# Two-block transformer on one core: the order of weight tiles in the mixers and in the output projection

## The chip, the cores and the metric

The kernel runs on one core of one Trainium2 chip, written in Bass with hand-placed semaphores. The metric is device time in microseconds of one execution; the median of three runs of the kernel before is 2701.41 us (2698.37 to 2704.88).

## The reference, cut to what matters

Two blocks of two layers each work on x of 256 tokens by 1024 features in float32. The change touches the token mixers of both. In each, three branches are weighted by gates, summed and projected:

```python
# first block, per layer (heads 8, head width 64; latent widths 256 and 128)
y_a = from_heads(moba_attention(partial_rope(qa), partial_rope(ka), va))
y_b = from_heads(stick_breaking_attention(qb_, kb_, vb_))
qc = to_heads(rms_norm(c_q, q_norm) @ w_uq, MLA_HEADS)
kv = to_heads(rms_norm(c_kv, kv_norm) @ w_ukv, MLA_HEADS)
kr = apply_rope(k_rope, cos_m, sin_m)              # one rotary key for all heads
y_c = from_heads(causal_softmax_attention(qc, concat(k_nope, kr), vc))
g = sigmoid(gates + b_gate)
merged = sum over n of g[n] * (y_n @ w_branch[n])
return merged @ w_out

# second block, per layer
o_b = rmsnorm(diff attention output, subln_g) * (1 - lambda_init)
u, v = gelu(uv);  v = rmsnorm(v, norm_g)
o_c = u * (einsum('gts,bnsgc->bntgc', tril(w_s), v) + b_s)   # the gating unit
mixed = gates[0] * (o_a @ w_branch_a) + gates[1] * (o_b @ w_branch_b) + gates[2] * (o_c @ w_branch_c)
x = x + mixed @ w_out
```

## The kernel before

Activations lie features by tokens: 128 partitions, 8 chunks of 256 tokens. Weights come as a stream of 360 tiles of 128x2048 (1 MB), built on the host in the order in which they are used (`weight_tiles`), through a ring of three slots. SyncE loads a slot as soon as VectorE is through with its last tile; ScalarE rounds the tile to its high part (`split_high`, L937), VectorE subtracts to get the low part (`split_low`, L1366), and TensorE makes three products for each block of 128x128: high by high, high by low, low by high (`blocks`, L374 to L376). A tile is 16 blocks, 48 matmuls over 256 tokens.

There is no scheduler. Each engine runs a program of its own, in the order written, and they meet on counted semaphores. `split_ahead` and `tile_done` let ScalarE and VectorE run up to three tiles ahead; both stand at fixed places in their programs. A projection (`project`, L419) takes the next tile and writes one of PSUM's banks 4 and 5 in turn (`open_fill`, L388); it waits until ScalarE has taken the bank's last result (`take`, L966; semaphore `pj_out`).

In the mixers, projections run beside attention steps. `sticks(beside)` (L512) is the stick-breaking attention: step s makes head s's scores, then calls `beside(s)`, then the running sums of head s-1 and the weighted values of head s-3. VectorE adds the sums (L1534) and the mask (L1541), ScalarE makes exp (L1046) and the log in three operations (L1052 to L1056). In step 0 comes the tile of the rotary key and the latent norms (high and low parts of the small operand, L1184 and L1764); in step 1 the query latent (`mla_w_uq`: four banks), and the rotation of the key, `kr`, held in `ff[64:96, 0, :]`; in step 2 the key/value latent (`mla_w_ukv`: six banks) and the first query rotation; in steps 3 to 8 the gate and branch tiles of branch 0 (`merge_gate`, `merge_branch`), with three more query rotations. A rotation is a matmul with a permutation to bank 6 (`rotate`, L437) and three VectorE operations (`rope`, L1465 to L1468), and it waits for the last rotation's `rope_done`. A branch result of half the features fills banks 6 and 7, and VectorE multiplies it by the gates held in `ff` (`merge_step`).

In the second block, behind the diff attention, come the norm of its output (two statistics, each two matmuls into bank 6, L896; ScalarE's `root`, L986 and L988; VectorE's scaling, L1911), the norm and products of the gating unit (L1916 and L903), and then the gate and branch tiles of branches 1 and 2.

The output projection (L571) multiplies four tiles by the merged input, whose second half of features is ready last (`merged_part`, L1583; semaphore `ml_ready`, counted once for each half). Its results lie in banks 0 to 3.

## Time and profile before

| | us |
|---|---|
| median of 3 runs | 2701.41 |
| profiled execution | 2703.62 |
| its span | 2702.0 |
| TensorE busy | 2451.9 |
| VectorE busy | 1662.1 |
| ScalarE busy | 1214.4 |

Mean granted clock of TensorE over the span: 0.946. The page lists busy time by engine, the waits name who held whom, the timeline shows single instructions with the idle time before them. The time in an idle bracket is counted from the end of the last instruction's record; matmuls overlap, so in dense code one starts before the last one's record ends.

### The profile page before, as it was taken

The numbers are of one execution on the slowest core, as the hardware profiler recorded it, in microseconds if no ns is written. First come the engines' busy times: TensorE is split into PE (matmuls) and PEld (weight loads), VectorE is DVE, ScalarE is ACT, GpSimd is POOL, SyncE is SP. The second block draws the span as 40 slices with busy tenths as digits, with TensorE's granted clock in tenths as the row PEclk, the third lists the DMA queues.
The fourth block names the chain that finished last, engine by engine and source line by source line (L and its number), as shares of the span: only waits on it lengthen the run. The fifth ranks groups of instructions, "written<-read, shape, count | busy, mean of one in ns | idle before, by whom it ended". The sixth has DMA issues, their size and how long they took to land.

```text
span 2702.0 us, 43597 instructions
## 1 busy us (share of the span) xinstructions
PE 2451.9 (91%) x16380; PEld 2198.0 (81%) x16380; DVE 1662.1 (62%) x2378; ACT 1214.4 (45%) x1574; POOL 73.4 (3%) x141
## 2 busy tenths in 40 slices
PE   3998989979979989899799898989899889988998
PEld 2997978869968978788789787679799876888897
DVE  6876656656768776665565554445655555555654
ACT  3444455444444444554344454354444443454443
POOL 0100000000000000000000000000000000000000
PEclk9998989989999999999999987899999988989999
DMA  7775544436647764444345433134455331334452
GB/s 302 276 277 174 185 164 163 163 122 220 246 171 250 277 235 156 173 155 159 138 156 186 171 127 108 63 125 162 160 182 183 139 141 63 126 125 156 170 181 100
DMA packets 74141, 461.52 MB, mean 171 GB/s; under 512 B 8272, under 2 KB 8416, under 8 KB 27648
## 3 DMA queue, kind: packets, MB, share of 16 engines
q1 hardware_dynamic: 53424, 384.33, 39.8%
q0 software_dynamic: 19120, 70.43, 7.4%
q10 hardware_dynamic: 1440, 4.62, 0.4%
q8 instruction: 104, 1.70, 0.3%
q14 instruction: 53, 0.43, 0.1%
HBM read 458.30 MB, written 1.05 MB: 170 GB/s over the span
## 4 chain that ended last, share of the span: by engine, by line
PE 85%; DVE 6%; ACT 4%; issue 3%; DMA 1%; DVEq 1%; ACTq 0%; SPq 0%
PE ps L594 19%; PE ps L374 16%; PE ps L375 16%; PE ps L376 16%; PE ps L596 9%; PE ps L431 2%; PE ps L491 1%; PE ps L442 1%; PE ps L458 1%; DMA set_a<-in_ada 1%; PE ps L471 1%; PE ps L457 1%; ACT whi L937 1%; DVE wlo L1366 1%; DVE x L1451 1%
## 5 line engine op out<-in xcount | busy, mean ns | idle before, releaser
L1366 DVE TENSOR_TENSOR wlo<-raw,whi 128x2048 fp32r<-128x2048 f32 x360 | 824.4, 2291 | 321.1 <-ACT whi L937 301.4
L937 ACT ACTIVATE whi<-raw 128x2048 fp32r<-128x2048 f32 x360 | 687.5, 1910 | 295.4 <-PE ps L376 292.1
L594 PE MATMUL ps<-hx,whi 128*128 128x512 f32 x2112 | 764.7, 405 | 33.0 <-DVE hx L1439 27.6
L596 PE MATMUL ps<-hx,wlo 128*128 128x256 f32 x2112 | 597.8, 283 | 0.0
L374 PE MATMUL ps<-hx,whi 128*128 128x256 f32 x1680 | 504.1, 300 | 27.0 <-DVE hx L1583 14.5
L594 PEld LDWEIGHTS ps<-hx,whi 128*128 128x128 f32 x2112 | 400.7, 190 | 141.8 <-DVE hx L1439 38.4
L375 PE MATMUL ps<-hx,whi 128*128 128x256 f32 x1680 | 486.9, 290 | 0.0
L376 PE MATMUL ps<-hx,wlo 128*128 128x256 f32 x1680 | 486.2, 289 | 0.0
L374 PE MATMUL ps<-yhi,whi 128*128 128x256 f32 x1440 | 408.5, 284 | 0.0
L375 PE MATMUL ps<-ylo,whi 128*128 128x256 f32 x1440 | 407.5, 283 | 0.0
L376 PE MATMUL ps<-yhi,wlo 128*128 128x256 f32 x1440 | 407.3, 283 | 0.0
L596 PEld LDWEIGHTS ps<-hx,wlo 128*128 128x128 f32 x2112 | 404.3, 191 | 0.0
L374 PEld LDWEIGHTS ps<-hx,whi 128*128 128x128 f32 x1680 | 333.1, 198 | 47.8 <-DVE hx L1583 15.3
L375 PEld LDWEIGHTS ps<-hx,whi 128*128 128x128 f32 x1680 | 334.1, 199 | 4.6 <-issue 4.4
L376 PEld LDWEIGHTS ps<-hx,wlo 128*128 128x128 f32 x1680 | 333.7, 199 | 0.0
L374 PEld LDWEIGHTS ps<-yhi,whi 128*128 128x128 f32 x1440 | 275.8, 192 | 4.7 <-issue 1.4
L376 PEld LDWEIGHTS ps<-yhi,wlo 128*128 128x128 f32 x1440 | 276.1, 192 | 0.0
L375 PEld LDWEIGHTS ps<-ylo,whi 128*128 128x128 f32 x1440 | 276.0, 192 | 0.0
L1391 DVE CUSTOM_DVE_ANT_0 adat<-adat,cact 128x1024 f32<-128x1024 f32 x128 | 155.4, 1220 | 5.0 <-issue 4.5
L1110 ACT ACTIVATE set_b<-ps 128x512 f32<-128x512 f32 x66 | 39.5, 599 | 238.5 <-PE ps L596 238.5
L431 PE MATMUL ps<-set_a,const 128*128 128x256 f32 x136 | 48.3, 516 | 97.2 <-DVE set_a L1419 97.2
L431 PEld LDWEIGHTS ps<-set_a,const 128*128 128x128 f32 x136 | 32.6, 255 | 108.8 <-DVE set_a L1419 70.4
(245 smaller groups left out, 2602.5 us busy)
## 6 DMA issues: line engine op xcount, KB each, us to landing
raw<-in_w SPq DMA_DIRECT2D x360, 1024.0 KB, 4.8
adat<-in_ada POOLq DMA_DIRECT2D x128, 512.0 KB, 4.5
raw<-in_ada SPq DMA_DIRECT2D x4, 512.0 KB, 11.3
blk<-in_block POOLq DMA_DIRECT2D x2, 990.5 KB, 5.0
set_a<-in_ada SPq DMA_DIRECT2D x3, 512.0 KB, 25.1
raw<-in_ada ACTq DMA_DIRECT2D x2, 512.0 KB, 11.8
set_b<-in_ada ACTq DMA_DIRECT2D x2, 512.0 KB, 17.5
x<-in_x SPq DMA_DIRECT2D x1, 1024.0 KB, 18.6
```

The source lines that it names most:

```text
L374: mm(out_ap, sh, mh, start=start and first, stop=False, skip_group_check=skip)
L375: mm(out_ap, sh, ml, start=False, stop=False, skip_group_check=skip)
L376: last = mm(out_ap, sl, mh, start=False, stop=stop and end, skip_group_check=skip)
L431: last = mm(stat[:, 0, :], c("inv1024"), sq[:, i // 2 * 4 + i % 2, :], start=(i == 0), stop=(i == 3))
L442: mm(out_ap, perm, src, start=True, stop=True).then_inc(*T.counts("rot_ready"))
L457: mm(ps[:, bank, 0:128], ins.q(u, 0, 128), ins.k(u, 0, 128), start=True, stop=True)
L594: mm(ps[:, bank + i, :].rearrange("p (a s) -> p a s", a=2), whi[:, slot, col:col + P], hx[:, :, k, :], start=(k == 0), stop=False)
L596: last = mm(ps[:, bank + i, 0:S], wlo[:, slot, col:col + P], hhi[:, k, :], start=False, stop=(k == KD - 1))
L937: A(whi[:, slot, :], raw[:, slot, :], ACT.Copy).then_inc(*T.counts("hi_ready"))
L1110: A(gate_sum, ps[:, 4:6, S:2 * S], ACT.Copy).then_inc(*T.counts("gb_ready"))
L1366: tt(wlo[:, slot, :], raw[:, slot, :], whi[:, slot, :].bitcast(F32), ALU.subtract)\
L1391: nc.vector.tensor_tensor_reduce(adat[:, slot, :], adat[:, slot, :], cact[:, :], 1.0, 0.0, ALU.mult, ALU.add, out_ap).then_inc(*T.counts(" ...
```

## The change

Output projection, both blocks: the first-half products of tiles 0 and 1 (both column groups) are made before the wait for the merged input's second half; the second halves follow. The two column groups of a bank now form one accumulation, as `down` does it.

First block: the tile stream and the steps beside the stick-breaking attention are reordered to rotary key, gate, query latent, gate, key/value latent, branch. The query rotations move: 0 after the gate tile of step 3; 1, 2 and 3 inside the key/value latent. The rotary key is held in `merged[64:96, 7, :]`, since gate results now fill `ff` before it has been used.

Second block: one gate tile before the sub-norm's statistics and one after them; the second statistic goes to bank 7 and no longer waits for the first root; ScalarE and VectorE each split one weight tile ahead of the first root. The first two gate tiles of the later loop are left out.

```diff
--- before.py
+++ after.py
@@ -279,7 +279,7 @@
 
         pos_in = bufC[:, 0, 0:S].bitcast(I32)
         cq_raw = set_a[:, 12:15, :]
-        kr = ff[64:96, 0, :]
+        kr = merged[64:96, 7, :]
         gs = ff[:, :, :]
         a32 = ff[:, 2:4, :]
         gate_sum = set_b[:, 0:2, :]
@@ -569,17 +569,28 @@
                 pe.wait_ge(*T.nth("y_ready", T.n["pairs"]))
 
             def output_projection():
+                def part(i, slot, half):
+
+                    for j in range(2):
+                        last = blocks(acc[:, 2 * i + j, :],
+                                      [(whi[:, slot, k * 256 + j * P:k * 256 + (j + 1) * P],
+                                        wlo[:, slot, k * 256 + j * P:k * 256 + (j + 1) * P],
+                                        hhi[:, k, :], hlo[:, k, :]) for k in range(4 * half, 4 * half + 4)],
+                                      start=(half == 0 and j == 0), stop=(half == 1), skip=True)
+                    return last
+
+
+                pe.wait_ge(*T.next("ml_ready"))
+                slots = []
+                for i in range(2):
+                    slots.append(tile())
+                    part(i, slots[i], 0)
+                pe.wait_ge(*T.next("ml_ready"))
                 for i in range(4):
-                    slot = tile()
-                    for j in range(2):
-                        for half in range(2):
-                            if i == j == 0:
-                                pe.wait_ge(*T.next("ml_ready"))
-                            last = blocks(acc[:, 2 * i + j, :],
-                                          [(whi[:, slot, k * 256 + j * P:k * 256 + (j + 1) * P],
-                                            wlo[:, slot, k * 256 + j * P:k * 256 + (j + 1) * P],
-                                            hhi[:, k, :], hlo[:, k, :]) for k in range(4 * half, 4 * half + 4)],
-                                          start=(half == 0), stop=(half == 1))
+                    if i >= 2:
+                        slots.append(tile())
+                        part(i, slots[i], 0)
+                    last = part(i, slots[i], 1)
                     last.then_inc(*T.counts("tile_used"))
 
 
@@ -687,7 +698,11 @@
                         mm(stat[:, 1, :], c1("inv128"), sq[:, 2, :], start=True, stop=True)\
                             .then_inc(*T.counts("stat_ready"))
                         free6[0] = None
-                    elif s == 1:
+                    elif s in (1, 3, 6, 7):
+                        merge_gate()
+                        if s == 3:
+                            rotate_q(0)
+                    elif s == 2:
                         slot = tile()
                         wait_h(3)
                         for i in range(4):
@@ -702,7 +717,7 @@
                             last.then_inc(*T.counts("tile_used" if i == 3 else "part_ready"))
                         pe.wait_ge(*T.nth("pj_out", T.n["fills"] - 4))
                         rotate(c1("perm_mla")[64:96, 64:128], kr, ps[64:128, 6, 0:S])
-                    elif s == 2:
+                    elif s == 4:
                         slot = tile()
                         for i in range(4):
                             bank = open_fill()
@@ -712,6 +727,8 @@
                                               [(whi[:, slot, col:col + P], wlo[:, slot, col:col + P],
                                                 smallhi[:, 512:768], smalllo[:, 512:768])])
                             last.then_inc(*T.counts("part_ready"))
+                            if i == 1:
+                                rotate_q(1)
                         for t in range(2):
                             bank = open_fill()
                             wv = [w_[:, slot, 0:1024].rearrange("p (h c) -> p h c", c=P)[:, :, HD:P]
@@ -720,18 +737,11 @@
                                           [(smallhi[:, 512 + t * P:512 + (t + 1) * P],
                                             smalllo[:, 512 + t * P:512 + (t + 1) * P], wv[0], wv[1])])
                             last.then_inc(*T.counts("tile_used" if t == 1 else "part_ready"))
-                        rotate_q(0)
-                    elif s < 9:
-                        if s in (3, 4):
-                            rotate_q(s - 2)
-                        if s % 3 == 2:
-                            if s == 5:
-                                wait_bank6()
-                            merge_branch(0)
-                        else:
-                            merge_gate()
-                        if s == 4:
-                            rotate_q(3)
+                            rotate_q(2 + t)
+                    elif s in (5, 8):
+                        if s == 5:
+                            wait_bank6()
+                        merge_branch(0)
 
                 sticks(beside_sticks)
                 wait_pairs()
@@ -886,15 +896,15 @@
                             merge_gate()
 
                 attend(diff, beside_diff)
+                merge_gate()
                 wait_bank6()
-
                 for i in range(2):
                     pe.wait_ge(*T.next("sq_ready"))
-                    if i:
-                        pe.wait_ge(*T.nth("rstd_ready", T.n["stat_ready"]))
                     for j in range(2):
-                        last = mm(stat[:, j, :], c2("inv128"), sq_od[:, 2 * i + j, :], start=True, stop=True)
+                        last = mm(ps[:, 6 + i, j * S:(j + 1) * S], c2("inv128"), sq_od[:, 2 * i + j, :],
+                                  start=True, stop=True)
                     last.then_inc(*T.counts("stat_ready"))
+                merge_gate()
 
                 pe.wait_ge(*T.next("vs_ready"))
                 pe.wait_ge(*T.next("wt_ready"))
@@ -908,8 +918,9 @@
                 free6[0] = None
                 for n in (1, 2):
                     for half in range(2):
-                        merge_gate()
-                        merge_gate()
+                        if (n, half) != (1, 0):
+                            merge_gate()
+                            merge_gate()
                         if n == 2 and half == 0:
                             pe.wait_ge(*T.next("gl_ready"))
                         merge_branch(n)
@@ -980,10 +991,10 @@
             def use_exp_tanh():
                 act.preload_act_table_set("exp_and_others")
 
-            def root(n=1):
+            def root(n=1, bank=6):
 
                 act.wait_ge(*T.next("stat_ready"))
-                A(rstd[:, 0:n, :], stat[:, 0:n, :], ACT.Ln, bias=c("eps"))
+                A(rstd[:, 0:n, :], ps[:, bank, 0:n * S].rearrange("p (c s) -> p c s", c=n), ACT.Ln, bias=c("eps"))
                 act.drain()
                 A(rstd[:, 0:n, :], rstd[:, 0:n, :], ACT.Exp, scale=-0.5).then_inc(*T.counts("rstd_ready"))
 
@@ -1183,14 +1194,16 @@
                             act.wait_ge(*T.next("t2_ready"))
                             A(smallhi[:, i * S:(i + 1) * S], set_a[:, 4 + i, :], ACT.Copy)\
                                 .then_inc(*T.counts("hh_ready"))
-                    elif s == 1:
+                    elif s in (1, 3, 5, 6, 7, 8):
+                        merge_step({1: 0, 3: 1, 5: 2, 6: 0, 7: 1, 8: 2}[s], 0, s // 6, True)
+                    elif s == 2:
                         for i in range(4):
                             if i < 3:
                                 act.wait_ge(*T.next("part_ready"))
                             else:
                                 tile_done()
                             take(set_a[0:96, 2 * i:2 * i + 2, :], rows=96)
-                    elif s == 2:
+                    elif s == 4:
                         for i in range(4):
                             act.wait_ge(*T.next("part_ready"))
                             take(set_a[0:64, 8 + 2 * i:10 + 2 * i, :], rows=64)
@@ -1199,8 +1212,6 @@
                         tile_done()
                         take(vm[:, 1, :])
                         act.wait_ge(*T.next("kr_ready"))
-                    elif s < 9:
-                        merge_step(s % 3, 0, s // 6, True)
 
                 sticks(1, beside_sticks)
 
@@ -1319,8 +1330,9 @@
                 A(rsum[:, 0, :], rsum[:, 0, :], ACT.Ln, bias=c("eps"), scale=1.0 / 512)
                 act.drain()
                 A(rsum[:, 0, :], rsum[:, 0, :], ACT.Exp, scale=-0.5).then_inc(*T.counts("vr_ready"))
+                split_high()
                 for i in range(2):
-                    root(2)
+                    root(2, 6 + i)
                     for j in range(2):
                         act.wait_ge(*T.next("odt_ready"))
                         A(yhi[:, 1, 2 * i + j, :], odt[:, 2 * i + j, :], ACT.Copy, scale=lam[:, 5:6])\
@@ -1764,22 +1776,21 @@
                             tt(smalllo[:, i * S:(i + 1) * S], set_a[:, 4 + i, :],
                                smallhi[:, i * S:(i + 1) * S].bitcast(F32), ALU.subtract)\
                                 .then_inc(*T.counts("h_ready"))
-                    elif s == 1:
+                    elif s in (1, 3, 5, 6, 7, 8):
+                        merge_step({1: 0, 3: 1, 5: 2, 6: 0, 7: 1, 8: 2}[s], 0, s // 6, True)
+                        if s == 3:
+                            rope_q(0)
+                    elif s == 2:
                         tile_done(False)
                         T.n["pj_out"] += 4
                         rope(kr, kr, ps[64:96, 6, 0:S], cosm, sinm, rstd[64:96, 0, :])
                         nc.vector.tensor_copy(set_a[64:96, 8:16, :], over(kr, HEADS))\
                             .then_inc(*T.counts("kr_ready"))
-                    elif s == 2:
+                    elif s == 4:
                         tile_done(False)
                         T.n["pj_out"] += 6
-                        rope_q(0)
-                    elif s < 9:
-                        if s in (3, 4):
-                            rope_q(s - 2)
-                        merge_step(s % 3, 0, s // 6, True)
-                        if s == 4:
-                            rope_q(3)
+                        for i in (1, 2, 3):
+                            rope_q(i)
                     if s < 8:
                         last_modulation(8 + s)
 
@@ -1905,6 +1916,7 @@
                 v.wait_ge(*T.next("vq_ready"))
                 tt(rsum[:, 0, :], esum[:, :, 0], esum[:, :, 1], ALU.add).then_inc(*T.counts("vsum_ready"))
                 T.n["sq_ready"] += 2
+                split_low()
                 for i in range(2):
                     root()
                     for j in range(2):
@@ -2084,8 +2096,8 @@
                 down(j - 1)
         down(NJ - 1)
 
-    def merge(gates, g0, branch, n_):
-        for half in range(2):
+    def merge(gates, g0, branch, n_, halves=(0, 1)):
+        for half in halves:
             put(slab(gates, g0 + n_ * D + 512 * half))
             put(slab(gates, g0 + n_ * D + 512 * half + 256))
             put(slab(branch, 512 * half, 512))
@@ -2099,9 +2111,13 @@
         put(slab(w, c_q))
         put(slab(w, c_kv, P))
         put(slab(w, k_r - 64, 96))
+        put(slab(w, gates))
         put(slab(inp["mla_w_uq"][l], 0, HEADS * MLA_QK))
+        put(slab(w, gates + 256))
         put(slab(inp["mla_w_ukv"][l], 0, HEADS * P))
-        for b in range(3):
+        put(slab(inp["mix_w_branch"][l, 0], 0, 512))
+        merge(w, gates, inp["mix_w_branch"][l, 0], 0, (1,))
+        for b in (1, 2):
             merge(w, gates, inp["mix_w_branch"][l, b], b)
         for j in range(4):
             put(slab(inp["mix_w_out"][l], 256 * j))
```

## Rows read from the trace of the kernel before

**Rows 1.** Page, part 1: engine, busy us (share of the span), instructions.

```profile
PE 2451.9 (91%) x16380; PEld 2198.0 (81%) x16380; DVE 1662.1 (62%) x2378; ACT 1214.4 (45%) x1574; POOL 73.4 (3%) x141
```

**Rows 2.** Waits of PE, whole span: who <- releaser: us in total, times, longest.

```profile
PE ps L431 <- DVE set_a L1419: 97.2, 17, 28.6
...
PE ps L374 <- DVE hx L1583: 14.5, 4, 3.6
...
PE ps L374 <- ACT set_a L966: 9.0, 2, 4.5
```

**Rows 3.** Timeline, PE, output projection: start us, us, instruction, count [idle before <- releaser].

```profile
551.51 0.28 PE L375 MATMUL ps<-hx,whi 128*128 128x256 f32 x1
551.63 0.28 PE L376 MATMUL ps<-hx,wlo 128*128 128x256 f32 x1
555.53 0.39 PE L374 MATMUL ps<-hx,whi 128*128 128x256 f32 x1 [3.62 <-DVE hx L1583]
```

**Rows 4.** Windows: stretch, us, busy us (count) by engine, PEclk, DMA share, GB/s.

```profile
555.50:578.90 23.40, 23.36 (x180) 23.16 (x180) 10.97 (x10) 7.67 (x5) 0.53 (x1) 0.93 0.47 161
2466.20:2490.40 24.20, 24.11 (x180) 23.90 (x180) 9.23 (x5) 7.62 (x4) 0.00 (x0) 0.89 0.38 132
```

**Rows 5.** Timeline, DVE, around the output projection's start.

```profile
548.38 2.29 DVE L1366 TENSOR_TENSOR wlo<-raw,whi 128x2048 fp32r<-128x2048 f32 x1 [0.58 <-ACT whi L937]
...
554.25 1.23 DVE L1583 SCALAR_TENSOR_TENSOR hx<-merged,hx 128x1024 fp32r<-128x1024 f32 x1 [1.12 <-ACT hx L1090]
```

**Rows 6.** Timeline, PE, second block: end of attention to first branch tile.

```profile
1807.74 0.38 PE L492 MATMUL ps<-bufC,set_b 128*128 128x128 f32 x2
1810.13 1.13 PE L896 MATMUL ps<-set_a,blk 128*128 128x256 f32 x4 [2.01 <-ACT set_a L973]
1816.54 2.07 PE L896 MATMUL ps<-set_a,blk 128*128 128x256 f32 x4 [5.28 <-ACT rstd L988]
1821.67 3.79 PE L903 MATMUL ps<-blk,set_a 128*128 128x128 f32 x16 [3.06 <-DVE set_a L1916]
1825.11 0.56 PE L374 MATMUL ps<-hx,whi 128*128 128x256 f32 x1
1825.47 0.41 PE L375 MATMUL ps<-hx,whi 128*128 128x256 f32 x1
1825.68 0.41 PE L376 MATMUL ps<-hx,wlo 128*128 128x256 f32 x1
...
1837.21 0.28 PE L374 MATMUL ps<-yhi,whi 128*128 128x256 f32 x1
```

**Rows 7.** Timeline, ACT and DVE, the same stretch.

```profile
1804.47 2.29 DVE L1366 TENSOR_TENSOR wlo<-raw,whi 128x2048 fp32r<-128x2048 f32 x1 [4.41 <-ACT whi L937]
...
1815.11 0.68 ACT L986 ACTIVATE rstd<-ps,const 128x512 f32<-128x512 f32 x1
...
1820.75 0.87 DVE L1916 TENSOR_SCALAR set_a<-set_a,rsum 128x512 f32<-128x512 f32 x2
...
1828.63 2.29 DVE L1366 TENSOR_TENSOR wlo<-raw,whi 128x2048 fp32r<-128x2048 f32 x1 [0.17 <-issue]
```

**Rows 8.** Timeline, PE, stick-breaking attention of the first layer.

```profile
374.95 0.36 PE L374 MATMUL ps<-smallhi,whi 128*96 128x256 f32 x1 [3.20 <-DVE smalllo L1764]
...
390.95 0.58 PE L374 MATMUL ps<-smallhi,whi 128*128 128x256 f32 x1 [4.49 <-ACT set_a L966]
...
396.26 1.07 PE L442 MATMUL ps<-set_a,blk 32*64 32x512 f32 x2
...
399.66 0.61 PE L442 MATMUL ps<-set_a,blk 32*64 32x512 f32 x1 [0.41 <-DVE set_a L1468]
...
419.75 0.39 PE L374 MATMUL ps<-yhi,whi 128*128 128x256 f32 x1
```

**Rows 9.** Timeline, DVE and ACT, step 2 of the same attention.

```profile
386.91 0.56 DVE L1534 TENSOR_TENSOR bufA<-bufA,ps 128x384 f32<-128x384 f32 x1
...
390.32 1.05 ACT L966 ACTIVATE set_a<-ps 64x512 f32<-64x512 f32 x2
```

## Prediction

> **What bounds the kernel now.** I read the page's busy times first: TensorE is busy for 2451.9 of 2702.0 us [rows 1], so it sets the end and an edit is worth what it takes out of TensorE's 250 idle us, plus what the clock gives back. Then the waits of TensorE over the whole span [rows 2]: the largest group, 97.2 us before the mean over x, is a chain of norms that the change doesn't touch. Those that it touches are the output projection's second wait (14.5 us, 4 times) and, in each of the two layers of a block, three more: the sub-norm's second statistic waits 5.3 us for the first root [rows 6], and in the stick-breaking attention the latent projections wait 3.2 us for the small operand's low part [rows 8] and 4.5 for a bank to be taken (9.0 in both). Last I read the timeline around one of each, since a wait is only worth its length if the next thing is ready, and the granted clock behind it.
>
> **What an idle TensorE costs twice.** In dense code a 128x256 matmul follows the last one after 0.12 us (551.51 to 551.63, [rows 3]). The 180 matmuls behind the output projection's wait would then take 179 x 0.12 + 0.28 = 21.76 us; they took 23.36, at a mean clock of 0.93, and in the fourth place 24.11 at 0.89 [rows 4]. So a wait of 3.6 us is followed by a stretch at the lower level (1.2 of 2.4 GHz) that costs 1.6 us once or 2.35 in the fourth place. Where the wait goes, that goes too.
>
> **Part 1, output projection (4 places).** Before, 12 matmuls (first half of output tile 0, j = 0) run, then TensorE stands from 551.63 + 0.12 = 551.75 to 555.53, 3.78 us, for the second half of the merged input's low part [rows 3]. The change puts all 48 first-half matmuls of the first two weight tiles ahead of that wait: 36 more, 36 x 0.12 = 4.32 us. They end at 551.75 + 4.32 = 556.07, 0.54 us after the wait's end, so it is covered whole. What must hold: the second tile's low part. VectorE makes it from 548.38 to 550.67 and the merged half from 554.25 to 555.48 [rows 5]; TensorE wants the second tile at 550.32 + 24 x 0.12 = 553.2, so it is 2.5 us early. Nothing is added: the number of matmuls, and the banks that they use, stay; the tile that is handed back first is used up at 559.0 instead of 559.9, so the ring isn't held either. Gain: 4 x 3.78 = 15.1 us of waits, and 3 x 1.6 + 2.35 = 7.15 us of clock, **22.3 us**. Bounds: 15.1 (the low stretches reappear at the next work) to 22.3.
>
> **Part 2, gating unit of the second block (2 places).** Before: statistic 1 starts at 1810.13 after 2.01 us idle, statistic 2 at 1816.54 after 5.28, the gating products at 1821.67 after 3.06, gate tiles 1 and 2 at 1825.11, and the first branch tile at 1837.21 [rows 6]. After: TensorE is free at about 1808.05 (the last attention product starts at 1807.74 and dense code follows it 0.31 later). Gate tile 1 takes 48 x 0.12 = 5.8 us, to 1813.9; both statistics, now in two banks, need the squares (there by 1810.7) and no root between them: 8 instructions, 2.07 us for 4 at the low clock [rows 6], so 1.7 for 8 at the full one and up to 3.5 at the low one; to 1815.6. Gate tile 2 goes to 1821.4. The later of the two gate tiles was split by 1804.47 + 2.29 = 1806.8 [rows 7], ahead of all this.
> The side that gets longer is ScalarE and VectorE. The change lets each split one weight tile (1.91 and 2.29 us by the page's groups) ahead of the first root. ScalarE's Ln is at 1815.11 [rows 7], so it moves to 1816.9 and its Exp ends at 1818.3; VectorE's split, which needs ScalarE's, runs 1817.0 to 1819.25, so the first normed pair starts then, 2.7 us later than before. From there the chain of before again, without its wait for statistic 2: Ln at 1820.6, root at 1822.0, the second pair 1822.1 to 1822.7, the scaled values to 1823.6 (before, 1820.75 to 1821.62 [rows 7]). So the gating products wait until 1823.65: TensorE idles 2.25 us there instead of 3.06, and this is the new last wait. The products took 3.44 us at the low clock (1821.67 to 1825.11), so 1.75 at the full one; then the branch tile starts at 1825.4, against 1837.21, a gain of 11.8 us. The low parts that the branch needs end at 1825.2. If the clock is low behind the 2.25 us, the products cost 1.7 more and a piece of the next tile up to 1.6. I take 10.5 for each place, **21 us**; bounds 2 x 8.5 to 2 x 12. The split brought forward is free otherwise: before, it stood at 1828.63 [rows 7], behind the gating unit, and the following tiles (1829 to 1831, 1831 to 1833) stay just ahead of TensorE, which wants the first at 1831.2.
>
> **Part 3, latent projections in the stick-breaking attention (2 places).** Order before, by step: key rotary tile; query latent; key/value latent; then gate, gate, branch. After: rotary tile; gate; query latent; gate; key/value latent; branch. The same matmuls run between the end of step 1's scores (374.95 less the wait before it, 371.7) and the branch tile (419.75), so the difference of its start is the gain [rows 8]. Walking it by the rows of before: gate 1 fills 371.7 to 377.5, over the 3.20 us wait. The running sums and scores end at 379.35, the query latent's first two banks (12 matmuls each) at 382.2. The third bank needs ScalarE's first take, and ScalarE makes it behind its own step: argument, exp, masked scores, three-op log. From VectorE's argument (386.91) to the end of the first take (390.32 + 0.59 = 390.91) that is 4.0 us [rows 8, 9]. VectorE reaches the argument at 380.4 (tile split to 379.15, modulation unit 1.2), the take ends at 384.4: a wait of 2.3 us that wasn't there. The key rotation and the next step end at 389.7, gate 2 at 395.5. VectorE rotates query 0 and does its unit, so the argument of step 4 is at 400.3 and the first key/value take ends at 404.3; TensorE has done two banks and a rotation by 401.5 and waits 2.8 (before 4.49). The query rotations 2 and 3 now sit inside that tile, and one follows another by 3.40 at the least (396.26 to 399.66 [rows 8]), since each waits until VectorE is through the last: waits of 0.4 and 1.8. The branch tile starts at 414.0. That is 5.75 us less if the clock stays up; gaps of 2.3 and 2.8 us with rotations around them should leave one or two low stretches, 2 us. **3.75 each, 7.5 us**; bounds 0 (three low stretches and a take 1 us later) to 11.5. The moved rotary key is the same copy and rotation to another place in SBUF, and its copy ends (390.6) long before it is read: nothing. Seven query, key and gate tiles change places in the stream of 1 MB loads, whose landing takes 4.8 us by the page; each is issued when the slot's low part is done, and the latest, that of the branch tile, lands some 20 us ahead: nothing.
>
> **Sum.** 22.3 + 21 + 7.5 = 50.8 us. The profiled execution took 2703.62 us, 1.6 over its span; this gives 2652.8 for it, and **2651** against the median of 2701.41.
>
> **Rivals.** (a) Part 3 brings nothing, because the ScalarE to VectorE chain comes last in both latent steps, and the smaller gaps leave as many low stretches as before. For it: my walk already finds 7.3 us of gaps where 8.1 stood. With part 2 at its lower bound of 17 us it gives 22.3 + 17 = 39.3, so 2662. Chance 0.25. (b) The gaps that are left don't lower the clock: the wait of 2.01 us before statistic 1 still had its matmuls at short spacing (4 in 1.13 us). Then 22.3 + 23.6 + 11.5 = 57.4, so 2644. Chance 0.12. (c) **Slower.** The granted clock. The long waits become more and shorter ones, and if each then holds TensorE low through what follows, not for a stretch but for the whole step, part 3's 36 us of work and part 2's 17 us per layer run at 0.21 us (1825.47 to 1825.68, [rows 6]) for 0.12: (36 + 17) x 0.75 = 40 us a layer, 80 in all, against 50.8 gained: 2731. It decides from some 26 us of added loss per layer. Against it: dense tiles bring the clock back soon: the 96 matmuls from 1825.11 to 1837.21 take 12.1 us, 0.6 over 96 x 0.12 [rows 6]. Chance 0.015. The Trainium skill, "TensorE: Matmul & The Clock Gate", section "A second HAM failure mode: psum-queue depth-cycling", states the rule that speaks for (c): short idle times between groups of matmuls that cycle through banks can make the clock swing between its levels. Taken at its word it would leave 2731; the low stretches of this trace follow idle or sparse TensorE time only. (d) The change doesn't do what it says: TensorE doesn't reach the filler because a tile or bank isn't ready. It would cost part 2's gain and half of part 1, leaving 18: 2683. The splits speak against it [rows 5, 7]. Chance 0.015. The forecast keeps 0.6.
>
> **Range and chances.** Forecast's own range 2645 to 2658; with (a) and (b), **2642 to 2667**. A measurement of this kernel can tell about 0.2%, 5.4 us, from no change. Faster by more: 0.97 (forecast, a, b); within: 0.015; slower: 0.015.
>
> **What would show it.** Right: no wait on the merged low part in the output projection, and some 192 matmuls in 23.1 us there; the root's wait gone, one wait of 2 to 2.5 us before the gating products; in the latent steps no wait on the small operand's low part, two of 2 to 3 us on ScalarE's takes, one near 1.8 us on the third rotation; mean clock up from 0.946. Wrong if the gating products wait 4 us or more, if the takes come as late as before (4.5 us), or if low stretches appear inside the dense gate tiles.

## The result, and the profile after

The changed kernel takes a median of 2656.0 us in four runs (2654.7 to 2663.0), beside 2701.1 us (2698.4 to 2704.9) for the kernel before on the same chip: a ratio of 0.9837, 95% interval 0.9816 to 0.9859, or 45 us less by the medians. (The ratios here and below are those on record with the runs; a quotient of medians can differ from them by 0.001.) The forecast was 2651 us, the range 2642 to 2667. The profiled execution is the longest of the four: 2663.0 us, its span 2661.4, against 2703.62 and 2702.0 before. So the traces differ by 40.6 us, and the terms below are held against that, not against 45.

The changed kernel's page, part 1 (as [rows 1]), and its waits of PE over the span (as [rows 2]):

```profile
PE 2448.2 (92%) x16380; PEld 2189.4 (82%) x16380; DVE 1660.7 (62%) x2378; ACT 1212.6 (46%) x1574; POOL 73.0 (3%) x141
```

```profile
PE ps L431 <- DVE set_a L1431: 97.2, 17, 28.7
...
PE ps L374 <- ACT set_a L977: 8.5, 4, 2.4
...
PE ps L913 <- DVE set_a L1928: 4.4, 2, 2.2
...
PE ps L442 <- DVE set_a L1480: 2.0, 2, 1.3
```

The output projection's wait (14.5 us, 4 times, in [rows 2]) has no row any more. What is left of the three parts is what the forecast's walk left: two waits of 2.2 us before the gating products, four on ScalarE's takes of the latent results, and two on a rotation. TensorE is busy for as long as before (2448.2 us against 2451.9), so nearly all that was won is idle time.

**Output projection**, timeline of PE, and the row of VectorE that was waited for before (against [rows 3, 5]):

```profile
547.97 0.28 PE L374 MATMUL ps<-hx,whi 128*128 128x256 f32 x1
...
553.73 0.28 PE L374 MATMUL ps<-hx,whi 128*128 128x256 f32 x1
...
573.16 0.67 PE L431 MATMUL ps<-set_a,const 128*128 128x256 f32 x2 [1.99 <-DVE set_a L1431]
```

```profile
551.91 1.22 DVE L1595 SCALAR_TENSOR_TENSOR hx<-merged,hx 128x1024 fp32r<-128x1024 f32 x1 [1.13 <-ACT hx L1101]
```

The low part of the merged input's second half is ready at 553.13; the second halves begin at 553.73, when the 48 first halves are through, without an idle bracket. The wait is covered with 0.6 us to spare.

**Gating unit**, timeline of PE in the first layer, of its last row in the second, and of ACT and DVE (against [rows 6, 7]):

```profile
1798.35 0.60 PE L491 MATMUL ps<-bufC,set_b 128*128 128x256 f32 x2
...
1804.75 1.89 PE L904 MATMUL ps<-set_a,blk 128*128 128x256 f32 x8
...
1814.60 2.05 PE L913 MATMUL ps<-blk,set_a 128*128 128x128 f32 x16 [2.21 <-DVE set_a L1928]
1816.40 0.37 PE L374 MATMUL ps<-yhi,whi 128*128 128x256 f32 x1
...
2363.29 3.68 PE L913 MATMUL ps<-blk,set_a 128*128 128x128 f32 x16 [2.21 <-DVE set_a L1928]
2366.63 0.45 PE L374 MATMUL ps<-yhi,whi 128*128 128x256 f32 x1
```

```profile
1806.17 1.91 ACT L948 ACTIVATE whi<-raw 128x2048 fp32r<-128x2048 f32 x1
1807.98 0.67 ACT L997 ACTIVATE rstd<-ps,const 128x512 f32<-128x512 f32 x1
...
1808.11 2.29 DVE L1378 TENSOR_TENSOR wlo<-raw,whi 128x2048 fp32r<-128x2048 f32 x1 [4.48 <-ACT whi L948]
...
1813.66 0.88 DVE L1928 TENSOR_SCALAR set_a<-set_a,rsum 128x512 f32<-128x512 f32 x2
```

Both statistics run as one group of 8, and the root comes behind the split on ScalarE. The same stretch in the kernel before begins in the first layer, and begins and ends in the second, at

```profile
1807.30 0.60 PE L491 MATMUL ps<-bufC,set_b 128*128 128x256 f32 x2
...
2373.07 0.60 PE L491 MATMUL ps<-bufC,set_b 128*128 128x256 f32 x2
...
2403.35 0.28 PE L374 MATMUL ps<-yhi,whi 128*128 128x256 f32 x1
```

From the last L491 group to the branch tile it is 18.05 us in the first layer (before, 1807.30 to 1837.21: 29.91) and 19.59 in the second (from 2347.04; before, 30.28), where the same 16 gating products take 3.34 us to the next tile instead of 1.80, at the low clock.

**Latent projections**, timeline of PE (against [rows 8]):

```profile
381.52 0.36 PE L374 MATMUL ps<-smallhi,whi 128*96 128x256 f32 x1 [1.88 <-ACT set_a L977]
...
401.70 0.58 PE L374 MATMUL ps<-smallhi,whi 128*128 128x256 f32 x1 [2.36 <-ACT set_a L977]
402.51 0.41 PE L374 MATMUL ps<-smallhi,whi 128*128 128x256 f32 x1
...
405.84 1.96 PE L442 MATMUL ps<-set_a,blk 32*64 32x512 f32 x2
...
410.04 1.94 PE L442 MATMUL ps<-set_a,blk 32*64 32x512 f32 x2 [0.65 <-DVE set_a L1480]
...
415.38 1.22 PE L518 MATMUL ps<-set_b 64*128 64x256 f32 x2
...
416.96 0.58 PE L374 MATMUL ps<-yhi,whi 128*128 128x256 f32 x1
```

The three waits have the places and nearly the lengths of the walk. What it lacked is the clock. Behind 401.70 each group of three matmuls takes 0.64 us (402.51 to the next at 403.15), and a pair of rotation matmuls (405.84) 1.96 instead of the 1.07 of [rows 8]: the lower of the two levels, 1.2 of 2.4 GHz. It stays low until the branch tile has run for 4 us (at 421.4 a group takes 0.36 again), some 20 us in all.

**The windows** of PE show it by stage: us, busy us (count) of PE, PEld, DVE, ACT, POOL, then granted clock, DMA share and GB/s. First two output projections, then the two gating units, then the two latent stages (from the second step's scores to the branch tile behind the sixth's):

```profile
547.90:571.10 23.20, 23.20 (x194) 23.07 (x193) 15.03 (x14) 10.00 (x6) 0.53 (x1) 1.00 0.62 210
2424.40:2447.70 23.30, 23.29 (x195) 23.09 (x193) 13.22 (x8) 10.00 (x6) 0.00 (x0) 1.00 0.53 185
1798.30:1816.40 18.10, 15.89 (x126) 15.42 (x125) 7.91 (x14) 13.65 (x27) 0.00 (x0) 1.00 0.33 117
2347.00:2366.60 19.60, 17.39 (x126) 16.92 (x125) 7.91 (x14) 15.16 (x27) 0.00 (x0) 0.92 0.31 108
368.00:417.00 49.00, 44.11 (x238) 33.46 (x237) 34.16 (x49) 26.55 (x41) 2.64 (x5) 0.83 0.42 149
1123.20:1172.40 49.20, 43.63 (x237) 34.12 (x236) 34.17 (x49) 26.48 (x41) 2.63 (x5) 0.86 0.39 139
```

And the latent stages of the kernel before, which the rows ahead of the prediction don't cover as a window:

```profile
370.80:419.70 48.90, 40.80 (x237) 33.39 (x236) 32.70 (x46) 26.05 (x41) 2.12 (x4) 0.90 0.38 137
1126.20:1174.50 48.30, 40.21 (x237) 33.04 (x236) 32.68 (x46) 26.04 (x41) 2.12 (x4) 0.89 0.40 145
```

The same work, with TensorE 3.3 us longer "busy" and as much less idle: the waits that went were paid back at the clock.

### The profile page after: what moved, and what is told of

The parts are those of the page before. It is cut to its first block, busy times and chain, and to the rows that moved or that the text cites. A ratio compares the mean times of both kernels' runs of the same rounds, so it can differ in the third digit from the quotient of the medians.

```text
span 2661.4 us, 43595 instructions
## 1 busy us (share of the span) xinstructions
PE 2448.2 (92%) x16380; PEld 2189.4 (82%) x16380; DVE 1660.7 (62%) x2378; ACT 1212.6 (46%) x1574; POOL 73.0 (3%) x141
## 4 chain that ended last, share of the span: by engine, by line
PE 86%; DVE 5%; ACT 4%; issue 3%; DMA 1%; DVEq 1%; ACTq 0%; SPq 0%
PE ps L605 19%; PE ps L374 16%; PE ps L375 15%; PE ps L376 15%; PE ps L607 9%; PE ps L431 2%; PE ps L491 1%; PE ps L442 1%; PE ps L458 1%; DMA set_a<-in_ada 1%; PE ps L471 1%; PE ps L457 1%; ACT whi L948 1%; DVE x L1463 1%; PE ps L492 1%
## 5 line engine op out<-in xcount | busy, mean ns | idle before, releaser
L605 PEld LDWEIGHTS ps<-hx,whi 128*128 128x128 f32 x2112 | 400.7, 190 | 141.8 <-DVE hx L1451 38.4
L374 PE MATMUL ps<-hx,whi 128*128 128x256 f32 x1680 | 498.8, 297 | 13.0 <-DVE hx L1451 5.4
L375 PE MATMUL ps<-hx,whi 128*128 128x256 f32 x1680 | 481.5, 287 | 0.0
L374 PEld LDWEIGHTS ps<-hx,whi 128*128 128x128 f32 x1680 | 327.4, 195 | 30.3 <-issue 10.5
L375 PEld LDWEIGHTS ps<-hx,whi 128*128 128x128 f32 x1680 | 328.5, 196 | 4.5 <-issue 4.4
## 6 DMA issues: line engine op xcount, KB each, us to landing
raw<-in_ada ACTq DMA_DIRECT2D x2, 512.0 KB, 11.8
```

Source lines behind the costliest of these rows:

```text
L374: mm(out_ap, sh, mh, start=start and first, stop=False, skip_group_check=skip)
L375: mm(out_ap, sh, ml, start=False, stop=False, skip_group_check=skip)
L605: mm(ps[:, bank + i, :].rearrange("p (a s) -> p a s", a=2), whi[:, slot, col:col + P], hx[:, :, k, :], start=(k == 0), stop=False)
```

## The experiments

The theory (A) was: parts 1 and 2 give what was forecast; part 3 gives nothing, because its smaller waits still bring the clock down, and now in a stage of small matmuls where that costs more. Its rival (B): part 3 gives its 7.5 us, and the missing microseconds are lost elsewhere. The first four runs do one part each, and one takes part 3's waits away. Each batch of runs has its own median of the kernel before: 2699.17, 2700.82 and 2699.54 us.

**One part alone: the output projection.** The kernel before with only `output_projection` of the change.

```diff
+                pe.wait_ge(*T.next("ml_ready"))
+                for i in range(2):
+                    slots.append(tile())
+                    part(i, slots[i], 0)
+                pe.wait_ge(*T.next("ml_ready"))
```

> The kernel before with the output projection's new order alone. Both theories: the wait for the merged low part and the low clock behind it go in all four places, 5.4, 5.4, 5.4 and 6.1 us in the profiled execution, together 22.3, so 2679 against 2701. A ratio of 0.9917. If it gives less than 18 us, the reordered work has a price that the stage does not show.

Measured: 2682.56 us, ratio 0.9943 (0.9927 to 0.9958), 16.6 us less. From the first of its 192 matmuls to the mean over x each place gains what it gains in the whole change: 5.37, 5.37, 5.38 and 6.16 us, 22.3 in all. So the stage is as forecast, and by the medians some 6 us are lost outside it. The windows of the norms behind two of these stages show a part of it: first the kernel before, then this one.

```profile
577.90:612.00 34.10, 21.80 (x95) 16.22 (x94) 20.29 (x34) 17.21 (x27) 0.00 (x0) 0.85 0.19 63
1332.60:1367.00 34.40, 22.22 (x92) 16.90 (x91) 20.17 (x33) 16.76 (x26) 0.00 (x0) 0.80 0.18 62
```

```profile
568.30:602.40 34.10, 22.09 (x92) 16.48 (x91) 20.16 (x33) 16.60 (x26) 0.00 (x0) 0.70 0.17 62
1319.30:1353.70 34.40, 22.39 (x93) 16.81 (x93) 20.25 (x34) 17.15 (x27) 0.00 (x0) 0.70 0.18 64
```

The same norm code, at a granted clock of 0.70 instead of 0.85 and 0.80. From the first mean to the second it takes 9.91 us instead of 9.40 in the first place, and in the five such stages together 2.5 us more. No edit touches them. The rest of the loss stands in no trace: this profiled execution is the fastest of its six, 24.6 us below the profiled one of before, and 4.9 us of that come from the second block's first layer between its first norm and its output projection (339.8 us before, 334.9 here), which no edit touches either.

**One part alone: the gating unit.**

```diff
                 attend(diff, beside_diff)
+                merge_gate()
                 wait_bank6()
...
-                    if i:
-                        pe.wait_ge(*T.nth("rstd_ready", T.n["stat_ready"]))
...
+                merge_gate()
```

> The kernel before with the second block's part alone (gate tiles around the statistics, statistic 2 in bank 7, one tile split ahead of the first root). From the changed kernel's profile: 11.8 us less in the first layer's stretch, 10 to 12 in the second's, together 22 to 24, so 2678. Rival: the wait of 2.2 us that is left before the gating products keeps the clock low in some executions, and the gain is 19 to 20.

Measured: 2681.94 us, ratio 0.994 (0.9923 to 0.9956), 17.2 us less. Timeline of PE, first layer:

```profile
1817.70 3.68 PE L903 MATMUL ps<-blk,set_a 128*128 128x128 f32 x16 [2.21 <-DVE set_a L1919]
1821.11 0.39 PE L374 MATMUL ps<-yhi,whi 128*128 128x256 f32 x1
```

The wait of 2.21 us stands where it was forecast, and here the clock is low behind it in both layers: 19.66 us to the branch tile (from 1801.45), as in the second layer of the whole change. That is a gain of 10.3 us in the first layer and 10.7 in the second (2357.77 to 2377.38). Some 3.7 us of these 20.9 do not reach the median. The profiled execution (2679.57) doesn't show the loss, being 24 us below the profiled one of before, so what took them is not settled.

**One part alone: the latent projections.** The tile stream, the rotary key's place and the steps of the first block; of the edit, the two gate tiles in the stream:

```diff
+        put(slab(w, gates))
         put(slab(inp["mla_w_uq"][l], 0, HEADS * MLA_QK))
+        put(slab(w, gates + 256))
         put(slab(inp["mla_w_ukv"][l], 0, HEADS * P))
```

> The kernel before with the latent part alone (tile order, gate tiles between the latent projections, rotations inside the key/value latent, rotary key moved). Theory A, from the changed kernel's profile: the waits fall from 8.1 to 4.9 or 5.6 us in a layer, but rotations, takes and short waits leave TensorE sparse and the clock low for 10 to 20 us, so a layer gains nothing or loses 2: 2699 to 2705. Theory B, my forecast: 7.5 us gained, 2694, and what was missing from the forecast lies elsewhere in the clock.

Measured: 2699.88 us, ratio 1.0005 (0.9992 to 1.0018), twelve runs from 2691.9 to 2710.5. No gain (the interval leaves room for 2 us), and not the 7.5 of theory B: theory A. Its profile holds both outcomes. Timeline of PE in the first layer, and the windows of the stage in both:

```profile
383.15 0.36 PE L374 MATMUL ps<-smallhi,whi 128*96 128x256 f32 x1 [1.88 <-ACT set_a L965]
...
403.35 0.39 PE L374 MATMUL ps<-smallhi,whi 128*128 128x256 f32 x1 [2.36 <-ACT set_a L965]
```

```profile
369.70:412.20 42.50, 36.83 (x234) 29.35 (x233) 31.78 (x45) 25.04 (x39) 2.11 (x4) 1.00 0.46 163
1118.60:1167.50 48.90, 44.02 (x234) 33.84 (x233) 33.19 (x46) 25.04 (x39) 2.11 (x4) 0.81 0.41 149
```

The same two waits as in the changed kernel, to a hundredth, and in the first layer the clock stays up: from the second step's scores to the sixth's 42.47 us, against 48.08 before. In the second layer of the same execution it falls, and the stretch takes 48.88 us and the two steps behind it 2.56 more. So up to the eighth step the order is worth 5.6 us a layer if the clock holds and costs up to 4 if it doesn't.

**The waits of part 3 taken away.** In steps 2 and 4 ScalarE takes the first latent bank before its own exp and the second one before it waits for the masked scores, so that TensorE's third bank is free; and the query rotations 2 and 3 move out of the key/value latent to steps 6 and 7.

```diff
             for s in range(HEADS + 3):
                 split_ahead()
+                early(s, 0)
...
                     A(bufC[:, u % 2, :], bufA[:, u % 2, :], ACT.Exp).then_inc(*T.counts("w_ready"))
+                early(s, 1)
...
                     elif s in (1, 3, 6, 7):
                         merge_gate()
+                        if s >= 6:
+                            rotate_q(s - 4)
...
-                            rotate_q(2 + t)
                     elif s in (5, 8):
-                        if s == 5:
-                            wait_bank6()
+                        wait_bank6()
```

> The changed kernel, with ScalarE taking the first two banks of each latent tile ahead of its exp and its log instead of behind them, and with query rotations 2 and 3 moved out of the key/value latent to behind the gate tiles of steps 6 and 7. Theory A (the takes and the rotations set these stages, and the low clock follows the waits that they leave): the waits of 1.9 and 2.4 us and that of 0.7 to 1.3 before the third rotation go, and so do low stretches of 10 to 15 us in a layer, worth 5 to 7: 8 to 10 us a layer, 2656 becomes 2638 to 2642. Theory B (the walk was right and the low stretches are chance): only the waits go, 4.5 us a layer, 2647. Rival C: the chain of exp and log gets later by the two takes (0.6 us each), and TensorE waits for the running sums instead: no change, 2656.

Measured: 2638.63 us, ratio 0.9775 (0.9759 to 0.9791), below either kernel. Windows of the two latent stages and their last wait on a take:

```profile
367.50:403.20 35.70, 34.96 (x233) 29.77 (x232) 29.38 (x42) 25.62 (x41) 2.11 (x4) 1.00 0.55 196
1109.30:1145.00 35.70, 34.96 (x233) 29.78 (x232) 29.37 (x42) 25.64 (x41) 2.11 (x4) 1.00 0.57 197
```

```profile
399.13 0.50 PE L374 MATMUL ps<-whi,smallhi 128*128 128x512 f32 x1 [0.74 <-ACT set_a L977]
```

The stage takes 34.8 us instead of 47.3, at the full clock; the next two steps take 18.1 instead of 19.5, with two rotations more in them. Of the 12.5 us in the first layer 4.8 are the clock (47.3 against the 42.5 of the layers in which it held), 4.8 are waits (those of a layer in which it held, 1.88 + 2.36 + 1.33, less 0.74), and the rest is mostly the two pairs of rotation matmuls that now run later.

**Only the early takes** (the two calls of `early` in the diff above), and **only the spread rotations** (its second half), to see which of the two it is.

> The changed kernel with ScalarE's early takes alone; the three query rotations stay inside the key/value latent. Theory (takes and rotations each set a wait): the waits of 1.9 and 2.4 us go, those for the rotations stay and grow, since TensorE reaches them 2 us earlier and VectorE does not: one wait of 2 to 3 us more in the key/value latent, some 3 to 5 us gained per layer with part of the low clock, 2647. Rival (the takes were all of it, the rotations cost nothing): as the version with both edits, 2639.

Measured: 2653.15 us, ratio 0.9815 (0.9797 to 0.9832). The waits on the takes are gone but for one of 0.74 us, and the rotations are late instead, since VectorE (L1490) has not finished the one before:

```profile
403.76 1.04 PE L442 MATMUL ps<-set_a,blk 32*64 32x512 f32 x2 [1.73 <-DVE set_a L1490]
...
407.03 1.94 PE L442 MATMUL ps<-set_a,blk 32*64 32x512 f32 x2 [0.93 <-DVE set_a L1490]
```

The second pair takes 1.94 us for the first one's 1.04: two waits, 1.73 and 0.93 us, and the clock is low again through the end of the step. 42.7 and 42.9 us for the stage.

> The changed kernel with query rotations 2 and 3 moved to behind the gate tiles of steps 6 and 7, and the takes left where they are. Theory: the waits of 1.9 and 2.4 us stay, the wait of 0.7 to 1.3 before the third rotation goes, and TensorE's work between the waits gets denser behind the key/value latent, so the long low stretch shortens: 3 to 4 us gained per layer, 2649. Rival (only the takes count): 2656.

Measured: 2653.94 us, ratio 0.9817 (0.98 to 0.9834). Both waits on the takes stand (1.87 and 2.36 us). The stage takes 39.8 us in the first layer and 42.5 in the second, with 3.4 and 10.2 us at the low clock.

Against the changed kernel (0.9837, and 0.9845 when it ran again) each alone gives some 0.0025 of the ratio, 7 us; both together give 0.007, 18. In the stage itself it is 4.7 and 6.3 us a layer for each alone and 12.7 for both (means of the two layers, from 47.5). With the two steps behind it, in which the moved rotations run, it is 5.7, 7.5 and 13.8. So the two mostly add up. What both give over the sum (1.7 us a layer in the stage, 0.6 with the two steps) fits the clock, which is low for some of the stage while either kind of wait is left and nowhere once both are gone, but the medians can't tell 14 from 18. Nor does all of it arrive: from the eighth step's scores to the output projection the kernels with the moved rotations take 114.7 to 117.3 us, the changed kernel 112.8 and 113.1. They have a wait of 0.5 to 0.6 us on a rotation before a branch tile there, and some of them a low stretch more.

**The gating unit without the split brought forward.** The split on each engine ahead of the first root is left out. It is the only step that the change adds to that chain: without it the gating products should come earlier, and the branch tile's weights later.

```diff
-                split_high()
                 for i in range(2):
                     root(2, 6 + i)
...
-                split_low()
                 for i in range(2):
                     root()
```

> The changed kernel without the one weight tile that ScalarE and VectorE split ahead of the first root. My step: the split costs the norms 1.9 us and, through VectorE, 2.0 us at the gating products (wait of 2.2), but without it the branch tile of branch 1 is not split before VectorE is through with the gating unit, some 3.4 us after the products' end for the unit and 2.3 for the split: TensorE would wait 5 us there instead, net 3 to 4 us worse per layer with the clock behind it: 2663. Rival: ScalarE and VectorE fit the split in by themselves and the time stays at 2656 or falls by 2 a layer.

Measured: 2668.66 us, ratio 0.9874 (0.9858 to 0.989), 8 to 10 us over the changed kernel by the ratios. Timeline of PE:

```profile
1811.09 1.95 PE L913 MATMUL ps<-blk,set_a 128*128 128x128 f32 x16
1818.55 0.58 PE L374 MATMUL ps<-yhi,whi 128*128 128x256 f32 x1 [5.51 <-DVE wlo L1377]
```

The products come without a wait, and TensorE then stands 5.51 us for the branch tile's low part, which VectorE makes behind the gating unit. That is 21.34 us to the branch tile for 18.05 and 19.59, and 8.2 us in that tile at a clock that has fallen, for 5.8 and 5.9: 4.0 to 5.6 us a layer. The split costs 2.2 us where it stands and saves 5.5 later, with the clock behind it. Without it part 2 would still gain some 6 us a layer of its 10.5 to 12.

**Is the loss in the norms a matter of the clock?** The output projection alone, with 15 matmuls more in each place whose results nobody reads, so that the norms begin 1.8 us later behind as much more dense work.

```diff
+                    if i == 3:
+                        pe.wait_ge(*T.nth("pj_out", T.n["fills"]))
+                        for k in range(15):
+                            mm(ps[:, 4, 0:S], whi[:, slots[3], 0:P], hhi[:, 0, :], start=True, stop=True)
                     last = part(i, slots[i], 1)
```

> The output projection's new order alone, with 15 matmuls whose results are not used put into each output projection (1.8 us of TensorE in each of 4 places, 7.2 in all). Against 2682.6 for the new order alone, which was 5.7 us short of the 22.3 that its own stage gained, while the norms behind it ran with 17 to 20 us of low clock where the kernel before has 10 to 14. Theory (the low clock behind an idle stretch depends on when it falls, and the new order has moved it to a worse moment): 1.8 us later, the first norms after the output projection of the first block show 10 to 14 us of low clock again, and the total is 2684, only 1 to 3 above. Rival (the denser output projection itself brings the longer low stretch): still 17 to 20 us, and the total is 2690.

Measured: 2689.04 us, ratio 0.995 (0.9935 to 0.9965): 5 us slower than the output projection alone by the gains against their own medians of before (11.8 against 16.6), 2 us by the ratios, where the added matmuls take 4 x 15 x 0.12 = 7.2. The norms' windows:

```profile
575.40:609.50 34.10, 21.87 (x96) 16.29 (x95) 20.48 (x34) 17.38 (x27) 0.00 (x0) 0.85 0.18 61
1329.80:1364.20 34.40, 22.14 (x96) 16.53 (x95) 20.58 (x34) 17.48 (x27) 0.00 (x0) 0.85 0.17 60
```

The clock is back at 0.85, and the norm takes 9.40 us from mean to mean again, 3.1 us less in the five stages together. It is not the chance of one execution: the five norms take 47.3 to 47.9 us together in the three profiles with the old output projection and 47.3 here, but 49.8 to 52.3 in all ten with the new one. So the norms lose by what runs ahead of them and not by an edit of theirs; whether it is the later start or the 15 dense matmuls that undoes it, this run doesn't separate.

The time is another matter. By the medians 2 to 5 of the 7.2 us came back, but 2689 is nearer to the rival's 2690 than to the theory's 2684, and the profiled execution is 13.2 us above that of the output projection alone, where 7.2 less 3.1 would be 4.1. The other 9 us stand in stages that neither edit touches, among them 2.6 us in each layer of the first block between its first norm and its second attention step (116.3 to 118.9). Over the whole span the two profiles have the same time at the low clock, 306 and 307 us: here it was moved, not taken away.

**Four kernels together on one chip**: parts 1 and 2 without part 3 (the changed kernel with the diff of the latent projections undone), the changed kernel again, the version with the latent waits removed again, and the one behind it.

> The changed kernel without its latent part: output projection and gating unit as changed, latent projections, tile order and rotary key as before. Theory (the latent part gains nothing in this kernel, since the waits that it keeps hold the clock low): the same time as the changed kernel, within 3 us. Rival (my forecast's 7.5 us are there when the other parts are): 6 to 8 us slower than the changed kernel.

> The changed kernel again, unedited, on the chip of the other three, as their measure: ratio 0.984 to the kernel before, 2656 where the kernel before has 2700. Its latent stages should again show a low stretch of 10 to 20 us after the waits for the takes; if their length differs much from the profile at hand, it is the moment of the wait that sets it.

Measured: 2661.06 us, ratio 0.9854 (0.9835 to 0.9873), without part 3, and 2658.12, ratio 0.9845 (0.9831 to 0.986), with it: 3 us between medians, within the intervals, which would let part 3 as written give anything from -4 to 9 us in this kernel. That it doesn't give 7.5 rests on part 3 alone and on the traces.

The parts don't add up. Alone they give 16.6, 17.2 and -0.7 us by the medians (0.011 of the ratio), parts 1 and 2 together 38.5 (0.015), the whole 45 and 41 (0.016), which is more than the intervals allow for. The edited stages gain much the same alone and together, so the 8 to 12 us lie in stages that no edit touches; no run here shows which.

The second profile of the changed kernel has the two latent stages side by side:

```profile
367.60:417.30 49.70, 44.82 (x235) 34.51 (x235) 33.54 (x48) 25.73 (x41) 2.15 (x5) 0.81 0.40 145
1124.00:1167.30 43.30, 37.62 (x237) 29.95 (x236) 32.36 (x46) 25.75 (x41) 2.11 (x4) 1.00 0.44 159
```

One program, the same instructions and the same waits on the takes: 48.9 us at a clock of 0.81, 42.5 at 1.00. The two profiles of the changed kernel differ by 7.2 us, and the second layer's stage with its two steps by 7.3. Of the eight latent stages profiled with this order (this kernel twice, part 3 alone, and the one without the split) two kept the clock up.

> Early takes and spread rotations together, again, beside the changed kernel: 16 to 18 us less than it, 2639. With each edit alone giving 3 to 6 us (2653 and 2654), this is a repeat of the finding that the two together give more than their sum: if it is real, no low clock in the latent steps of either layer; if it was chance, some 10 us less than the changed kernel.

Measured: 2639.99 us, ratio 0.9771 (0.9755 to 0.9787), as before, and the clock stays at 1.00 in both latent stages again.

**The last wait before the gating products.** On top of that version VectorE scales the gating unit's input ahead of its split, since neither needs the roots.

```diff
+                v.wait_ge(*T.next("vr_ready"))
+                for t in range(2):
+                    last = ts(vg[:, t, :], vg[:, t, :], rsum[:, 0, t:t + 1], None, ALU.mult)
+                last.then_inc(*T.counts("vs_ready"))
                 split_low()
```

> The version with early takes and spread rotations, and in the second block VectorE scales the gating unit's values as soon as their root is there, ahead of its weight tile and of both normed pairs. My step said that VectorE's place in line, not the root, holds the gating products (wait of 2.2 us in each layer). Then they start as gate tile 2 ends, and TensorE waits for the branch's low parts instead, 1.1 to 1.3 us: 1 us a layer, 2 in all, below what the measurement tells, but the wait of 2.2 us on L1928's successor is gone from the profile. Rival (the root of the gating values is what comes last): the wait stays.

Measured: 2641.71 us, ratio 0.9788 (0.9775 to 0.9801), not told apart from the version without it. Timeline of PE:

```profile
1783.85 1.95 PE L913 MATMUL ps<-blk,set_a 128*128 128x128 f32 x16
1787.20 0.36 PE L374 MATMUL ps<-yhi,whi 128*128 128x256 f32 x1 [1.40 <-DVE ylo L1943]
```

The 2.21 us before the products are gone, and 1.40 us stand behind them, for the low part of the branch's input, which hangs on the same roots. From the last L491 group to the branch tile it is 17.23 us in both layers. The version without it took 18.06 where the clock held and 19.4 to 19.6 in the other three of its four profiled layers: 0.8 us gained in the one case, 2.2 to 2.4 in the other, and up to 5 in both layers is still not seen in the median. The chain of roots ends that stage, not the order of what hangs on it.

## Why the prediction was right, and where it was not

**Part 1 held to the tenth.** Forecast 22.3 us; the four places gain 5.37, 5.37, 5.37 and 6.15 us, 22.3 in sum (for instance 30.56 us before and 25.19 after, 547.97 to 573.16). Its 192 matmuls take 23.20 us at a clock of 1.00, where 23.1 was said. Both halves of the term, the wait and the clock behind it, were right: with no wait there is no low stretch.

**Part 2 held.** Forecast 21 us, measured 11.86 + 10.69 = 22.6. The step that carries it, a new last wait of 2.25 us before the gating products, was measured at 2.21 in both layers, its releaser the one named. The 10.5 for each place were a compromise between the clock held and not held; the two layers show one of each, 1.5 us apart. The first was luck: of the 16 such layers in all profiles that keep the wait of 2.21 us, two kept the clock through the products (18.06 us) and 14 took 19.1 to 19.7, so 10.7 a layer is the usual gain. That the split brought forward is free was right only in the sense that it saves more than its 2.2 us: without it 5.51 us of wait stand at the branch tile.

**Part 3 failed, by the price of the clock.** Forecast 7.5 us. The walk through the steps is good: 2.3, 2.8 and 1.8 us of waits were said, 1.88, 2.36 and 0.65 to 1.33 came, and where the clock holds the stage takes 42.5 us and gives 5.6, for the 5.75 of the walk. The step that failed is "should leave one or two low stretches, 2 us". Where the clock falls, it is low for 17 to 24 us of the stage and the two steps behind it, in work of which half are small matmuls and rotations: the stage takes 47.3 to 48.9 us instead of 42.5 and the next two steps 2.1 to 2.6 more, 7 to 9 us instead of 2. In the profiled execution the stage and those steps lose 1.8 + 2.3 us; 2.9 come back between there and the output projection, where a low stretch of 3.4 us in dense gate tiles (from 457.5 in the first layer of before) has no counterpart. Net −1.2 us for both layers instead of +7.5. That is rival (a) for part 3 by its second reason, as many low stretches as before; its first, that the takes come last, was already in the forecast's own waits of 2.3 and 2.8 us. Part 2 did not fall to its lower bound, so the time did not reach (a)'s 2662.

**What no step of mine held.** Outside the three parts the profiled execution is 3.1 us longer (22.3 + 22.6 − 1.2 = 43.7 against 40.6). The norms of the first block are the plainest part of it: four of the five that come behind an edited stage take 0.61 to 0.94 us more from mean to mean. The output projection alone shows the same loss (2.5 us, clock 0.70 for 0.85), and 15 more matmuls in front of them undo it.

The sum closes: the forecast's 50.8 us less 8.7 for part 3 and 3.1 outside, plus 1.6 for part 2, is 40.6. That is the profiled execution, the slowest of four. The median's 45 us are 4.5 more, and no trace of that batch says where; that the median (2656.0) fell within the forecast's own 2645 to 2658, when part 3 and the stages outside fell 12 us short of it in the trace, is in part luck.

**The rivals.** (b), a clock that doesn't fall, came true in two gating units of 16 and two latent stages of eight; all at once, never. (d) did not occur: tiles and banks were ready. (c) did not either. Its mechanism, shorter waits that hold TensorE low through a whole step, is what part 3 shows in six of eight stages; its scale is not, since the dense tiles behind it restored the clock within 4 us of the branch tile. The Trainium skill, "TensorE: Matmul & The Clock Gate", section "A second HAM failure mode: psum-queue depth-cycling", says that where groups of matmuls cycle through PSUM banks, short idle times between them make the clock swing between its two levels. Six of the eight latent stages agree (waits of 1.88 and 2.36 us, a clock of 0.81 to 0.87 over the stage), two with the same waits stay at 1.00, and so do the six stages with one wait of 0.7 us.

## What to carry over

A wait replaced by two shorter ones of half the length isn't half won: read the granted clock of the stage that follows each, and price the low case by the work that would run in it, small matmuls and all, not by a fixed toll. Work moved in front of a wait pays in full where the filler is dense and covers the wait whole, as in the output projection. Where several waits each can bring the clock down, also try the version with all of them gone: here it is the only version in which the stage keeps the full clock in both layers, in each of its three profiles.

## What the runs showed of the hardware

- The clock at the same waits is not the same from one layer or execution to the next: 42.5 or 48.9 us for one stage of one program, with waits of 1.88 and 2.36 us in both. What decides it these runs don't show.
- The granted clock of a stage that no edit touches changes with what runs ahead of it: 0.85 and 0.80 in the norms' windows before, 0.70 with the output projection's new order, 0.85 with 15 dense matmuls (1.8 us) more in it.
- A wait of 2.21 us was followed by 16 matmuls in 1.80 us in one layer and 3.34 in the other; over 16 profiled layers, twice in 1.8 and otherwise in 2.8 to 3.4.
